# Pooled products one by one between the last pair's states; three output units ahead of the last pair, the fourth behind it

## The chip, the cores and the metric

The kernel runs on one core of one Trainium2 chip, as one program. The metric is the device time of one execution in microseconds. The core's engines are TensorE (PE in the rows; PEld is its weight load), VectorE (DVE), ScalarE (ACT), GpSimd (POOL) and SyncE (SP), which issues the transfers. They run side by side and meet at semaphores only.

## The reference, cut to what matters

Two transformer blocks run on 512 tokens of 1024 channels. The second block has a mixing layer whose input is split in two: 512 channels go through a recurrence over the sequence with 8 heads of 64 (`rwkv7_time_mix`), and 512 channels through averages over windows of 2, 4, 8 and 16 tokens (`multiscale_pool_mix`). Both halves are joined and multiplied by `w_out`, and the result is added to x. A feed-forward layer follows.

```python
    pooled = jnp.stack(outs, axis=2)
    mixed = jnp.einsum('bsgc,gcd->bsgd', pooled, w_pool.astype(f32))
    return (mixed.reshape(B, S, POOL_WIDTH) * pool_scale).astype(p.dtype)
...
        x = x + jnp.concatenate([y_rw, y_pool], axis=-1) @ w_out[l]
        x = x + 0.5 * swiglu(rms_norm_2(x, ffn2_norm[l]), ffn2_w_gate[l], ffn2_w_up[l], ffn2_w_down[l])
```

## The kernel before

**Units.** All large weights come as 233 units of 128x1024 float32 numbers (512 KB) through a ring of four slots. SyncE loads unit u to `raw`. ScalarE writes its rounded part to `w_hi` (`high_n`, L622, signals `hi_done`). GpSimd writes the rest to `w_lo` in four parts (`low`, L457, signals `lo_done`). TensorE then multiplies in three products, hi by hi, hi by lo and lo by hi (`three`, L1558 to L1560), and gives the slot back with `unit_used`. For `w_out`, unit U_OUT + m holds all weights of output tile m (128 output channels), in eight 128x128 blocks, one for each input tile k. `out_block(m, k, ...)` is one block, so three products of 128x512, that add up in PSUM bank m % 4.

**Input tiles of w_out.** Tiles k = 0 to 3 are the four pairs of heads of the recurrence. Tiles 4 to 7 are the four pool groups. Each is needed as `act_hi` (ScalarE: `mix_hi`, `pool_hi`) and `act_lo` (VectorE: `mix_lo`, `pool_lo`).

**The pairs.** The recurrence is worked out for pairs 0 to 3, in two lanes: pairs 0 and 2 in PSUM banks 0 to 3, pairs 1 and 3 in banks 4 to 7. `pair(p)` is written for each engine as a generator with 20 steps. Its steps 10 to 15 are the six states S1 to S6: TensorE multiplies (L1974), VectorE adds (L1444), and each state needs the one before it. Then come Y (L1978), the mean (L1982), the variance (L1986) and its spread over the channels, bc (L1991), between which VectorE and ScalarE work (`yc`, `sq`, `sd`, `inv`, `wide`, `yn`, `out`). Then `mix_hi(3)` and `mix_lo(3)` make input tile 3.

**Order of the work.** `in_turns` interleaves the lanes on each engine by hand. When the even lane has ended, the odd lane (pair 3) has its steps 11 to 20 left, and behind each of them the engine takes one step of its own generator `closing()`. What is left of `closing()` then runs on. On TensorE, `closing()` first issues the four products `w_pool` by `pooled` (float32, 128x512, L2019) behind step 11, which is S2. Its next three steps are empty. Then come the 28 blocks of units U_OUT to U_OUT + 3 for all k but 3, one behind each step of pair 3 and the rest in a row. Then TensorE closes the four units with k = 3, which needs pair 3, and goes on with units U_OUT + 4 to U_OUT + 7, eight blocks each. Unit U_OUT + 4 takes the slot of unit U_OUT.

ScalarE's `closing()` begins with the wait for pair 2's `out`, and prepares the units U_OUT to U_OUT + 2 behind `pool_hi(3)`. GpSimd's `closing()` (unchanged) makes the low parts of units U_OUT to U_OUT + 3 as they come, from the moment at which pair 3's step "Nb" is done. The pair's own buffers lie in the slots, so these units can't be written earlier. Behind the pairs, VectorE's `x2_new(m)` adds tile m to x once `unit_used` says that it is closed, ScalarE squares it (`x2_square`), and only then does ScalarE's queue come to `high_n(U_OUT + m + 4)`.

Of the kernel before, what the change touches and what calls it, by code (L numbers as in the profile page):

```python
# [21 lines left out]
KT = D // P  # L22
# [9 lines left out]
PAIRS = RW // P  # L32
CH = 64
NCH = T // CH
# [26 lines left out]
U_OUT = U_IN + len(IN_STARTS)  # L61
# [3 lines left out]
RING = 4  # L65
# [58 lines left out]
class Buffers:  # L124


    def __init__(self, bank, AA, MBR, MK, BT, KT, VT, GH, MT, TT, X, S, RP, OV):
# [5 lines left out]
PE_STEPS = (["tA", "tB", "tK", "tV", "LR", "K0", "K1", "AVa", "AVb", "G1a", "G1b", "Wa", "Wb", "GHa", "GHb", "RP", "OV", "MTa", "MTb", "Na", "Nb"]  # L133
            + [f"S{c}" for c in range(1, NCH - 1)] + ["Y", "mean", "var", "bc"])
VE_STEPS = (["LRa", "LRb", "K0a", "K0b", "K1a", "K1b", "AVb", "G1b", "Wb", "GHb", "RP", "MTa", "MTb", "Na", "Nb"]
            + [f"S{c}" for c in range(1, NCH - 1)] + ["Y", "yc", "inv", "yn", "out"])
# [11 lines left out]
def at(steps, pair, name):  # L148

    return pair // 2 * len(steps) + steps.index(name) + 1  # L150


LAG = 10
AHEAD_OF_SOLVE = 4


def in_turns(pair_program, closing):
# [8 lines left out]
    for first in (even, odd):  # L166
        for _ in range(AHEAD_OF_SOLVE):
            next(first)
    for _ in range(LAG):
        next(even)  # L170
# [8 lines left out]
def build(nc, a_vec, a_const, a_mask, a_x, a_xt, a_cs, a_wmod, a_w, a_lora, a_pool, out):  # L179
# [5 lines left out]
    with ExitStack() as ctx:  # L185
# [45 lines left out]
        def v(name, i=0, n=1):  # L231
            return vec[:, VEC[name] + i:VEC[name] + i + n]
# [92 lines left out]
        def sem(name):  # L325
            if name not in sems:
                sems[name] = ctx.enter_context(nc.semaphore(name))
            return sems[name]
# [18 lines left out]
        tensor_step, vector_step, scalar_step, pool_step = ([sem(f"{e}_step{i}") for i in range(2)] for e in ("tensor", "vector", "scalar", "pool"))  # L347
# [17 lines left out]
        def _(sp):  # L365
# [12 lines left out]
            def load_wm(i):  # L378

                n, flag, _, before = wm_place[i]  # L380
                if before is not None:
                    sp.wait_ge(sem("wm_used"), before + 1)
                sp.dma_start(wm_buf(n), a_wmod[i]).then_inc(wm_full[flag], 16)
# [229 lines left out]
        def _(act):  # L613
            def after(s, n):
                act.wait_ge(s, n)

            def high(u, slot, turn, first=False):

                act.wait_ge(raw_full[slot], 16 * (turn + 1))
                if not first:  # L620
                    act.wait_ge(unit_used, u - RING + 1)
                nc.scalar.activation(w_hi[:, slot, :], raw[:, slot, :], ACT.Copy).then_inc(hi_done, 1)  # L622

            def high_n(u):
                if u < NU:
                    high(u, u % RING, u // RING, u < RING)
# [304 lines left out]
            def mix_hi(p):  # L931
                nc.scalar.activation(act_hi[:, p, :], rG[:, p, :], ACT.Copy).then_inc(sem("mix_hi"), 1)

            def pool_hi(g):
                after(sem("pool_mm"), g + 1)
                nc.scalar.activation(act_hi[:, PAIRS + g, :], ps[:, g, :], ACT.Copy, scale=v("pool_scale", g)).then_inc(sem("pool_hi"), 1)

            def closing():

                act.wait_ge(vector_step[0], at(VE_STEPS, PAIRS - 2, "out"))  # L940
                mix_hi(0)

                act.wait_ge(vector_step[1], at(VE_STEPS, PAIRS - 3, "out"))
                mix_hi(1)
                yield
                mix_hi(2)
                pool_hi(0)
                yield
                pool_hi(1)
                pool_hi(2)  # L950
                yield

                act.wait_ge(tensor_step[1], at(PE_STEPS, PAIRS - 1, "OV"))
                assert U_OUT % RING == 3
                pool_hi(3)
                for u in range(U_OUT, U_OUT + RING - 1):
                    high_n(u)
                    yield
                act.wait_ge(vector_step[1], at(VE_STEPS, PAIRS - 1, "Y"))
                high_n(U_OUT + RING - 1)  # L960

            in_turns(pair, closing)
            act.wait_ge(vector_step[1], at(VE_STEPS, PAIRS - 1, "out"))
            mix_hi(PAIRS - 1)
# [47 lines left out]
        def _(ve):  # L1012
# [10 lines left out]
            def tt(o, a, b, op, name=None):  # L1023
                chain(nc.vector.tensor_tensor(o, a, b, op), name)  # L1024

            def stt(o, a, s, b, op0, op1, name=None):
                chain(nc.vector.scalar_tensor_tensor(o, a, s, b, op0, op1), name)  # L1027
# [440 lines left out]
            def mix_lo(p):  # L1468
                after(sem("mix_hi"), p + 1)
                tt(act_lo[:, p, :], rG[:, p, :], act_hi[:, p, :].bitcast(f32), SUB, "mix_lo")  # L1470

            def pool_lo(g):
                after(sem("pool_hi"), g + 1)
                stt(act_lo[:, PAIRS + g, :], ps[:, g, :], v("pool_scale", g), act_hi[:, PAIRS + g, :].bitcast(f32), MUL, SUB, "pool_lo")

            def closing():
                yield
                mix_lo(0)
                mix_lo(1)
                yield  # L1480
                mix_lo(2)
                pool_lo(0)
                yield
                pool_lo(1)
                pool_lo(2)
                yield

                ve.wait_ge(tensor_step[1], at(PE_STEPS, PAIRS - 1, "Nb"))
                pool_lo(3)

            in_turns(pair, closing)
            mix_lo(PAIRS - 1)

# [43 lines left out]
            n = 0  # L1537
# [16 lines left out]
        def _(pe):  # L1554
            after = pe.wait_ge

            def three(o, wh, wl, xh, xl, start, stop, **check):
                nc.tensor.matmul(o, wh, xh, start=start, stop=False, **check)  # L1558
                nc.tensor.matmul(o, wh, xl, start=False, stop=False, **check)  # L1559
                return nc.tensor.matmul(o, wl, xh, start=False, stop=stop, **check)  # L1560

            def blk(slot, b):
                return w_hi[:, slot, b * P:(b + 1) * P], w_lo[:, slot, b * P:(b + 1) * P]
# [432 lines left out]
            def out_block(m, k, start, stop):  # L1996

                u = U_OUT + m
                if start:
                    after(lo_done, u + 1)  # L2000
                    if m < RING:
                        after(sem("pool_lo"), m + 1)
                    else:
                        after(sem("x2_new"), m - 3)
                if m == 0:
                    after(*((sem("mix_lo"), k + 1) if k < PAIRS else (sem("pool_lo"), k - PAIRS + 1)))
                last = three(ps[:, m % 4, :], *blk(u % RING, k), act_hi[:, k, :], act_lo[:, k, :], start, stop)
                if stop and m < KT - 1:
                    last.then_inc(unit_used, 1)
                return last  # L2010


            others = [k for k in range(KT) if k != PAIRS - 1]

            def closing():
                after(sem("pooled"), len(WINDOWS))
                pe.wait_ge(vector_step[0], at(VE_STEPS, PAIRS - 2, "out"))
                for g in range(len(WINDOWS)):
                    nc.tensor.matmul(ps[:, g, :], w_pool[:, g, :], pooled[:, g, :], start=True, stop=True).then_inc(sem("pool_mm"), 1)  # L2019
                for _ in range(4):  # L2020
                    yield

                n = 0
                for m in range(RING):
                    for k in others:
                        out_block(m, k, k == 0, False)
                        n += 1
                        if n < NCH - 1 or n % 5 == 0:
                            yield

            in_turns(pair, closing)


            for m in range(KT - 1):
                if m >= RING:
                    for k in others:
                        out_block(m, k, k == 0, False)
                out_block(m, PAIRS - 1, False, True)
            for k in range(KT):
                out_block(KT - 1, k, k == 0, k == KT - 1).then_inc(sem("act_free"), 1)  # L2040
# [81 lines left out]
```

## Time and profile before

| | us |
|---|---|
| runs: median (lowest to highest) | 1588.21 (1586.77 to 1591.11) |
| profiled execution: its time | 1597.47 |
| profiled execution: its span | 1595.7 |
| PE, DVE, ACT, POOL busy | 1499.1, 565.7, 508.6, 761.8 |
| mean granted TensorE clock | 0.969 |

The span runs from the first to the last instruction of the profiled execution; 1.8 us of its time lie outside it. All positions in the rows are us from the start of the span. The clock is a share of full speed: 1.00 is 2.4 GHz and 0.50 is 1.2 GHz.

### The profile page before, as it was taken

What the parts mean: (1) busy time and instruction counts of PE and PEld (TensorE: products, weight loads), DVE (VectorE), ACT (ScalarE), POOL (GpSimd) and SP (SyncE); (2) the same over time, 40 slices, a digit from 0 to 9 for tenths busy, and PEclk for the clock granted to TensorE, in tenths of its full rate; (3) what the DMA queues carried; (4) which work ended last, traced back from release to release, by engine and by line L of the source; (5) the groups of instructions that cost most, each with busy time, mean ns of one, the idle gap of its engine ahead of it and who ended that gap; (6) DMA issues with size and microseconds to landing.
All of it is one profiled execution on the core that took longest, in us unless ns stands there. A gap on an engine that the chain in (4) does not pass through costs nothing.

```text
span 1595.7 us, 20172 instructions
## 1 busy us (share of the span) xinstructions
PE 1499.1 (94%) x7230; PEld 1237.9 (78%) x7230; DVE 565.7 (35%) x794; ACT 508.6 (32%) x706; POOL 761.8 (48%) x1013
## 2 busy tenths in 40 slices
PE   5797999999999999999999999689889999999997
PEld 4674788888888788888888687578667888888887
DVE  6795342222003832222001647845523322222003
ACT  4424333333123333223222664122313322322112
POOL 0372464555555655455455636160034745545553
PEclk9888999999999999999999999899879999999999
DMA  8871234222222232232232221000012323223221
GB/s 310 318 264 40 93 132 145 98 96 96 97 100 79 93 105 92 92 105 92 96 102 92 72 73 63 9 2 1 1 53 93 117 94 105 91 93 105 93 79 53
DMA packets 44545, 156.90 MB, mean 98 GB/s; under 512 B 4944, under 2 KB 7376, under 8 KB 44240
## 3 DMA queue, kind: packets, MB, share of 16 engines
q1 hardware_dynamic: 44496, 156.22, 28.5%
q8 instruction: 33, 0.54, 0.1%
q14 instruction: 16, 0.13, 0.0%
HBM read 154.11 MB, written 2.10 MB: 98 GB/s over the span
## 4 chain that ended last, share of the span: by engine, by line
PE 77%; issue 11%; DVE 7%; POOL 4%; ACT 1%; DVEq 0%; POOLq 0%; ACTq 0%
PE ps L1558 23%; PE ps L1560 23%; PE ps L1559 23%; POOL w_lo L457 4%; DVE act_lo L1027 1%; DVE tri_p L1024 1%; DVE tri_x L1024 1%; PE ps L1918 1%; DVE xT L1027 1%; PE ps L1978 1%; DVE mid_sq L1027 0%; PE ps L1925 0%; PE ps L1931 0%; PE ps L1974 0%; PE ps L1965 0%
## 5 line engine op out<-in xcount | busy, mean ns | idle before, releaser
L457 POOL TENSOR_TENSOR w_lo<-raw,w_hi 128x256 fp32r<-128x256 f32 x932 | 694.3, 778 | 750.3 <-ACT w_hi L622 750.0
L1558 PE MATMUL ps<-act_hi,w_hi 128*128 128x512 f32 x1328 | 532.0, 401 | 20.5 <-DVE act_lo L1024 11.3
L1559 PE MATMUL ps<-act_lo,w_hi 128*128 128x512 f32 x1328 | 523.1, 394 | 0.0
L1560 PE MATMUL ps<-act_hi,w_lo 128*128 128x512 f32 x1328 | 522.9, 394 | 0.0
L622 ACT ACTIVATE w_hi<-raw 128x1024 fp32r<-128x1024 f32 x233 | 245.0, 1055 | 451.9 <-PE ps L1560 424.0
L1558 PEld LDWEIGHTS ps<-act_hi,w_hi 128*128 128x128 f32 x1328 | 253.3, 191 | 85.8 <-issue 14.9
L1559 PEld LDWEIGHTS ps<-act_lo,w_hi 128*128 128x128 f32 x1328 | 253.5, 191 | 53.9 <-issue 2.7
L1560 PEld LDWEIGHTS ps<-act_hi,w_lo 128*128 128x128 f32 x1328 | 253.0, 190 | 53.6
L1558 PE MATMUL ps<-hid_hi,w_hi 128*128 (+3 forms) x584 | 220.4, 377 | 9.0 <-DVE hid_lo L1027 5.9
L1559 PE MATMUL ps<-hid_lo,w_hi 128*128 (+3 forms) x584 | 219.9, 376 | 0.0
L1560 PE MATMUL ps<-hid_hi,w_lo 128*128 (+3 forms) x584 | 219.8, 376 | 0.0
L1558 PEld LDWEIGHTS ps<-hid_hi,w_hi 128*128 128x128 f32 x584 | 111.2, 190 | 29.3 <-issue 9.6
L1560 PEld LDWEIGHTS ps<-hid_hi,w_lo 128*128 128x128 f32 x584 | 111.1, 190 | 19.7
L1559 PEld LDWEIGHTS ps<-hid_lo,w_hi 128*128 128x128 f32 x584 | 111.2, 190 | 19.6
L717 ACT ACTIVATE hid_hi<-g_buf 128x512 f32 (+1 forms) x66 | 41.8, 633 | 257.9 <-DVE g_buf L1167 217.5
L1164 DVE TENSOR_TENSOR u_buf<-ps,rstd 128x512 f32<-128x512 f32 x44 | 30.4, 691 | 182.6 <-PE ps L1560 182.6
L1169 DVE TENSOR_TENSOR hid_lo<-g_buf,hid_hi 128x512 f32 (+1 forms) x66 | 48.1, 730 | 58.7 <-ACT hid_hi L717 58.7
L1162 DVE TENSOR_TENSOR g_buf<-ps,rstd 128x512 f32<-128x512 f32 x44 | 30.4, 691 | 94.0 <-PE ps L1560 93.6
L715 ACT ACTIVATE g_buf<-g_buf 128x512 f32<-128x512 f32 x66 | 41.1, 622 | 48.9 <-DVE g_buf L1154 37.3
L1152 DVE SCALAR_TENSOR_TENSOR g_buf<-ps,vec,g_buf 128x511 f32<-128x511 f32 x22 | 16.5, 750 | 108.2 <-ACT g_buf L713 108.2
L1027 DVE SCALAR_TENSOR_TENSOR xT<-ps,mods,xT 128x512 f32<-128x512 f32 x16 | 12.0, 751 | 113.9 <-PE ps L1560 113.5
L1523 DVE SCALAR_TENSOR_TENSOR xT<-ps,xT 128x256 f32<-128x256 f32 x16 | 6.8, 424 | 110.0 <-PE ps L1560 110.0
(264 smaller groups left out, 1150.9 us busy)
## 6 DMA issues: line engine op xcount, KB each, us to landing
raw<-weight_units SPq DMA_DIRECT2D x233, 512.0 KB, 3.2
wm_ring<-mod_units SPq DMA_DIRECT2D x16, 512.0 KB, 5.9
wm_mid<-mod_units SPq DMA_DIRECT2D x16, 512.0 KB, 6.6
wm_early<-mod_units SPq DMA_DIRECT2D x8, 512.0 KB, 9.3
wm_late<-mod_units SPq DMA_DIRECT2D x8, 512.0 KB, 5.4
x_tok<-tokens SPq DMA_DIRECT2D x4, 512.0 KB, 6.4
xT<-tokens_by_channel SPq DMA_DIRECT2D x1, 2048.0 KB, 14.9
result<-act_out SPq DMA_DIRECT2D x16, 128.0 KB, 1.8
```

The source lines that it names most:

```text
L457: ins = nc.gpsimd.tensor_tensor(w_lo[:, slot, c], raw[:, slot, c], w_hi[:, slot, c].bitcast(f32), SUB)
L622: nc.scalar.activation(w_hi[:, slot, :], raw[:, slot, :], ACT.Copy).then_inc(hi_done, 1)
L715: nc.scalar.activation(g_buf[:, q, :], g_buf[:, q, :], ACT.Silu).then_inc(s["silu"], 1)
L717: nc.scalar.activation(hid_hi[:, bass.ds(j * T, T)], g_buf[:, q, :], ACT.Copy).then_inc(s["hid_hi"], 1)
L1024: chain(nc.vector.tensor_tensor(o, a, b, op), name)
L1027: chain(nc.vector.scalar_tensor_tensor(o, a, s, b, op0, op1), name)
L1162: nc.vector.tensor_tensor(g, gate, rstd[:, :], MUL).then_inc(s["act_in"], 1)
L1164: nc.vector.tensor_tensor(u_, val, rstd[:, :], MUL).then_inc(s["val_read"], 1)
L1169: nc.vector.tensor_tensor(hid_lo[:, bass.ds(j * T, T)], g, hid_hi[:, bass.ds(j * T, T)].bitcast(f32), SUB).then_inc(s["hid_lo"], 1)
L1558: nc.tensor.matmul(o, wh, xh, start=start, stop=False, **check)
L1559: nc.tensor.matmul(o, wh, xl, start=False, stop=False, **check)
L1560: return nc.tensor.matmul(o, wl, xh, start=False, stop=stop, **check)
```

## The change

TensorE issues the four pooled products one by one, behind S2, S3, S4 and S5. It waits for pair 2's `yn` in place of its `out`. The blocks for k other than 3 are issued for three units only (`BEFORE_MIX = 3`, 21 blocks), two behind each step of pair 3 from S6 on. These three units are closed with k = 3, and the fourth is done behind them like the later ones, all of its eight blocks in a row. ScalarE prepares unit U_OUT first, U_OUT + 1 and U_OUT + 2 between the `mix_hi` and `pool_hi`, and U_OUT + 3 one step of pair 3 later than before: behind `sd`, no longer behind `sq`. VectorE's `mix_lo` and `pool_lo` are spread by one step each.

```diff
+BEFORE_MIX = 3
...
             def closing():
 
+                assert U_OUT % RING == 3
+                act.wait_ge(tensor_step[1], at(PE_STEPS, PAIRS - 1, "OV"))
+                high_n(U_OUT)
                 act.wait_ge(vector_step[0], at(VE_STEPS, PAIRS - 2, "out"))
                 mix_hi(0)
 
                 act.wait_ge(vector_step[1], at(VE_STEPS, PAIRS - 3, "out"))
                 mix_hi(1)
                 yield
+                high_n(U_OUT + 1)
                 mix_hi(2)
                 pool_hi(0)
                 yield
+                high_n(U_OUT + 2)
                 pool_hi(1)
+                yield
                 pool_hi(2)
                 yield
-
-                act.wait_ge(tensor_step[1], at(PE_STEPS, PAIRS - 1, "OV"))
-                assert U_OUT % RING == 3
                 pool_hi(3)
-                for u in range(U_OUT, U_OUT + RING - 1):
-                    high_n(u)
-                    yield
+                yield
+                yield
+                yield
                 act.wait_ge(vector_step[1], at(VE_STEPS, PAIRS - 1, "Y"))
                 high_n(U_OUT + RING - 1)
...
             def closing():
                 yield
                 mix_lo(0)
+                yield
                 mix_lo(1)
+                pool_lo(0)
                 yield
                 mix_lo(2)
-                pool_lo(0)
-                yield
                 pool_lo(1)
+                yield
                 pool_lo(2)
                 yield
-
                 ve.wait_ge(tensor_step[1], at(PE_STEPS, PAIRS - 1, "Nb"))
                 pool_lo(3)
...
             def closing():
                 after(sem("pooled"), len(WINDOWS))
-                pe.wait_ge(vector_step[0], at(VE_STEPS, PAIRS - 2, "out"))
+                pe.wait_ge(vector_step[0], at(VE_STEPS, PAIRS - 2, "yn"))
                 for g in range(len(WINDOWS)):
                     nc.tensor.matmul(ps[:, g, :], w_pool[:, g, :], pooled[:, g, :], start=True, stop=True).then_inc(sem("pool_mm"), 1)
-                for _ in range(4):
                     yield
 
-                n = 0
-                for m in range(RING):
-                    for k in others:
-                        out_block(m, k, k == 0, False)
-                        n += 1
-                        if n < NCH - 1 or n % 5 == 0:
-                            yield
+                for n, (m, k) in enumerate((m, k) for m in range(BEFORE_MIX) for k in others):
+                    out_block(m, k, k == 0, False)
+                    if n % 2:
+                        yield
 
             in_turns(pair, closing)
 
 
-            for m in range(KT - 1):
-                if m >= RING:
-                    for k in others:
-                        out_block(m, k, k == 0, False)
+            for m in range(BEFORE_MIX):
+                out_block(m, PAIRS - 1, False, True)
+            for m in range(BEFORE_MIX, KT - 1):
+                for k in others:
+                    out_block(m, k, k == 0, False)
                 out_block(m, PAIRS - 1, False, True)
```

## Rows read from the trace of the kernel before

**Rows 1.** The page: busy time, and the chain that ended last.

```profile
PE 1499.1 (94%) x7230; PEld 1237.9 (78%) x7230; DVE 565.7 (35%) x794; ACT 508.6 (32%) x706; POOL 761.8 (48%) x1013
...
PE 77%; issue 11%; DVE 7%; POOL 4%; ACT 1%; DVEq 0%; POOLq 0%; ACTq 0%
```

**Rows 2.** Stretches of the span: length, busy (instructions) per engine, clock, DMA.

```profile
core 0: us, PE busy (x) PEld busy (x) DVE busy (x) ACT busy (x) POOL busy (x), PEclk, DMA share, GB/s
1143.90:1147.56 3.66, 2.38 (x5) 1.35 (x6) 1.51 (x4) 1.67 (x3) 0.00 (x0) 0.54 0.00 0
1147.56:1150.97 3.41, 3.41 (x6) 1.34 (x5) 0.00 (x0) 1.37 (x2) 0.00 (x0) 0.50 0.00 0
1150.97:1154.38 3.41, 1.74 (x8) 0.88 (x6) 2.08 (x5) 2.99 (x4) 0.53 (x1) 0.99 0.00 0
1154.38:1157.13 2.75, 1.50 (x4) 0.93 (x4) 2.64 (x5) 1.22 (x2) 2.75 (x5) 0.51 0.01 3
1157.13:1168.60 11.47, 11.01 (x35) 8.03 (x34) 3.77 (x6) 1.58 (x2) 6.15 (x10) 0.50 0.42 139
1168.60:1174.86 6.26, 6.26 (x20) 5.00 (x21) 2.40 (x4) 1.35 (x3) 2.10 (x4) 0.50 0.25 84
1174.86:1192.35 17.49, 17.49 (x78) 14.30 (x76) 2.08 (x3) 1.23 (x3) 0.00 (x0) 1.00 0.00 0
1192.35:1196.25 3.90, 0.16 (x2) 0.00 (x1) 1.94 (x3) 3.25 (x5) 3.29 (x5) 0.89 0.00 0
1196.25:1202.30 6.05, 6.05 (x14) 4.79 (x15) 2.22 (x3) 1.90 (x3) 6.05 (x8) 0.51 0.47 146
1202.30:1215.50 13.20, 13.20 (x59) 10.89 (x58) 2.77 (x4) 3.17 (x4) 8.71 (x13) 1.00 0.38 133
```

**Rows 3.** TensorE's timeline: start, length, line, tiles, count, idle before and releaser.

```profile
1145.76 6.21 PE L2019 MATMUL ps<-pooled,w_pool 128*128 128x512 f32 x8
...
1156.36 0.80 PE L1974 MATMUL ps<-S,MT 128*128 128x128 f32 x2 [1.25 <-DVE S L1444]
...
1158.58 3.09 PE L1978 MATMUL ps<-RP,S 128*128 128x64 f32 x14
...
1163.35 2.08 PE L1982 MATMUL ps<-rB,const 128*128 128x512 f32 x2 [0.30 <-DVE rB L1450]
...
1170.02 2.05 PE L1991 MATMUL ps<-const,rK 128*128 128x128 f32 x8
...
1196.25 0.80 PE L1558 MATMUL ps<-act_hi,w_hi 128*128 128x512 f32 x1 [3.74 <-POOL w_lo L457]
```

**Rows 4.** ScalarE's timeline, same columns.

```profile
1135.95 0.62 ACT L927 ACTIVATE rK<-norms 128x512 f32<-128x512 f32 x1
...
1152.66 2.94 ACT L622 ACTIVATE w_hi<-raw 128x1024 fp32r<-128x1024 f32 x3
...
1166.72 1.04 ACT L622 ACTIVATE w_hi<-raw 128x1024 fp32r<-128x1024 f32 x1
...
1191.84 1.04 ACT L622 ACTIVATE w_hi<-raw 128x1024 fp32r<-128x1024 f32 x1
```

**Rows 5.** VectorE's timeline, same columns.

```profile
1144.05 0.69 DVE L1465 TENSOR_TENSOR rG<-rB,rG 128x512 f32<-128x512 f32 x1
...
1154.21 0.91 DVE L1024 TENSOR_TENSOR act_lo<-rG,act_hi 128x512 fp32r<-128x512 f32 x1
...
1175.07 0.69 DVE L1024 TENSOR_TENSOR act_lo<-rG,act_hi 128x512 fp32r<-128x512 f32 x1 [0.70 <-ACT act_hi L932]
1190.58 1.42 DVE L1024 TENSOR_TENSOR xT<-ps,xT 128x512 f32<-128x512 f32 x2 [14.81 <-PE ps L1560]
...
1218.80 6.56 DVE L1027 SCALAR_TENSOR_TENSOR act_lo<-xT,vec,act_hi 128x512 fp32r<-128x512 f32 x7 [0.87 <-ACT act_hi L974]
```

**Rows 6.** GpSimd's timeline, same columns.

```profile
1153.85 8.73 POOL L457 TENSOR_TENSOR w_lo<-raw,w_hi 128x256 fp32r<-128x256 f32 x12 [80.98 <-ACT w_hi L622]
...
1192.96 12.45 POOL L457 TENSOR_TENSOR w_lo<-raw,w_hi 128x256 fp32r<-128x256 f32 x16 [22.27 <-ACT w_hi L622]
```

More of the change, by code:

```diff
@@ L1478, in closing @@
                 mix_lo(0)
+                yield
                 mix_lo(1)
+                pool_lo(0)
                 yield
                 mix_lo(2)
-                pool_lo(0)
+                pool_lo(1)
                 yield
-                pool_lo(1)
                 pool_lo(2)
```

## The prediction

> **What bounds the kernel now.** I read the page first. TensorE is busy for 94% of the span and carries 77% of the chain that ended last [rows 1], so a change pays if it takes TensorE's idle time away or lets it run at the higher clock. Next I cut the stretch around the change into windows at the places where the granted clock changes [rows 2]. Three things are to be seen there. First, between 1150.97 and 1157.13 TensorE is busy for 1.74 + 1.50 = 3.24 of 6.16 us: it waits for VectorE's additions between the states S3 to S6 (1.25 us before S6 alone, [rows 3]). Second, from 1154.38 to 1174.86, 20.5 us, it runs at 0.50, so 1.2 GHz, although it is busy nearly throughout. Third, from 1192.35 to 1196.25 it waits for GpSimd's `w_lo` of unit U_OUT + 4 [rows 2, 3], and then runs at 0.51 for 6.05 us.
>
> What stands behind the clock can be read off the same rows. It fell to 0.5 when work became sparse (1143.9, 1154.4, and with the wait at 1192 to 1196). It rose twice behind gap-free stretches: at 1150.97, after TensorE had been busy without a gap since 1145.97 with the pooled products, and at 1174.86, after 6.26 us without a gap. In the 11.47 us before 1168.60 the small gaps sum to 0.46 us, and the small products of Y and of the variance lie in it [rows 2, 3]; it did not rise. By the Trainium skill, page "TensorE: Matmul & The Clock Gate", section "Part 1: The HAM clock gate", the default state is the lower clock and activity releases it; the trace agrees, and where a stretch falls decides which clock it gets.
>
> Prices: at full clock 17.49 us hold about 77 products, 0.227 each, 0.68 us for a block of three. At 1.2 GHz 6.05 us hold 14, 0.432 each, 1.30 us for a block [rows 2]. The four pooled products took 6.2 us, 5.0 of them at half clock and 1.0 at full [rows 2, 3], so 1.75 us each at half and 0.88 at full clock. Work at the other clock than in its row is halved or doubled (an estimate from these).
>
> **The change part by part.** *Wait on `yn` in place of `out`:* nothing. `out` ends at 1144.05 + 0.69 = 1144.74 [rows 5], and S2, which stands ahead of the products, waits for an addition that VectorE does behind it.
>
> *Pooled products between the states.* Each product (1.75 or 0.88 us) now covers the 0.35 us addition and its latency that TensorE waited for. I lay the new order out from S2. I let it start 0.3 us later than before, as ScalarE, idle from 1136.57 [rows 4], now makes w_hi of U_OUT at once, and GpSimd starts its low part at about 1142.3, beside VectorE's `out`. The row for such company is 0.91 us for an operation that takes 0.69 alone, and 6.56 us for seven that take 0.75 [rows 5]. By the Trainium skill, page "SBUF — State Buffer", section "Who interferes with whom", an instruction of VectorE with two SBUF inputs and one of GpSimd that reads SBUF block each other, the second waiting for the first; by full blocking each of the handful of such operations here would lose up to one GpSimd part, 12.45/16 = 0.78 us [rows 6], some 3 us in all. The rows show 0.2 to 0.4 each, and I take those.
>
> From 1146.3 at half clock: product 1.75, S3 0.5, product 1.75, S4 0.5, that is 1150.8, 4.5 us without a gap. I expect the clock to rise about here, near 1151. Then product 0.88 and S5 to 1152.1, product to 1153.0. S6 waits for the S5 addition, in front of which VectorE has S4's, `mix_lo(1)` and `pool_lo(0)`: 0.1 + 0.35 + 0.91 + 0.75 + 0.35 behind 1150.8, 1153.3. S6 to 1153.6, two blocks to 1155.0. Y waits for the S6 addition behind `mix_lo(2)` and `pool_lo(1)`, 1155.3, and takes half of 3.09 us: 1156.8. Two blocks 1158.2, mean (half of 2.08) 1159.2, two blocks 1160.6, variance 0.9, 1161.5, two blocks 1162.8. Then bc waits for ScalarE: `sd` 0.3, the w_hi of U_OUT + 3 that now stands there 1.04, `wide` 0.63, 1163.5; bc to 1164.5. Thirteen of the 21 blocks are left: 8.84 us, 1173.4.
>
> *Tile 3.* Before, `mix_lo(3)` ended at 1175.76, 5.7 us behind the start of bc at 1170.02 [rows 3, 5]. Now that would be 1169.2, 4.2 us ahead of need. So issuing only 21 blocks ahead of it costs nothing; without the 13 blocks it would cost 4.7 us.
>
> *Three units closed, the fourth behind them.* Closings 2.04 us, 1175.4; fourth unit 8 blocks, 5.44 us, 1180.8. Before, the w_lo of U_OUT + 4 came 3.3 (1196.25 less 1192.96) + 1.12 + 1.26 = 5.7 us behind the start of the first addition to x at 1190.58 [rows 3 to 6], and only four closings lay in between. Now the first closing ends at 1174.1, the addition starts at about 1174.3, w_lo is there at 1180.0, and the fourth unit covers all of it, with 0.8 us to spare. The idle 3.9 us go. So does what they brought: 6.05 us at half clock would take 3.0 at full. GpSimd needs 12.45/4 = 3.1 us a unit [rows 6], TensorE 5.44, so it does not fall behind later. The DMAs of the units behind U_OUT + 3 start earlier, when the low parts are done; the DMA share stays under 0.5 in these rows. *The three further units* 24 blocks, 16.3 us: 1197.1.
>
> **Sum.** In the profile of before unit U_OUT + 6 is closed at 1215.5, now at 1197.1: 18.4 us. Of it the stall is 3.9, the half clock behind it 3.0, and 11.5 come from the stretch up to 1192. All that follows depends on this end and is unchanged, so the gain reaches the end of the program. The profiled execution took 1597.5 us, 9.3 more than the median of the runs shown; I carry the difference over. The moment at which the clock rises will vary: each us that it comes later than 1151 costs about 0.42 us (18.4 less 8.3 of the first rival, over 24 us). I take it as 3 us late: 17 us, 1588.2 - 17 = **1571**.
>
> **The rivals.**
> *The clock stays low until 1174.86, as before.* For it speaks that the states' products are short and have their own waits, and that the broken stretch before 1168.60 did not raise the clock. Against it that pooled products and states follow each other without a gap from 1146.3 on. Then the order runs at half clock: products and states to 1155.3, two blocks 1157.9, Y 1160.9, blocks 1163.5, mean 1165.5, blocks 1168.1, variance 1169.9, blocks 1172.5, bc 1174.5. That is 8.3 blocks at 1174.86, where before had 32 - 17.49/0.68 = 6.3. The gain is 2 x 0.68 = 1.4, plus 3.9 and 3.0: 8.3 us, 1580.
> *It rises somewhere in the blocks (1157 to 1168)*, which are now less broken: 8.3 + 0.42 x (6 to 18) = 11 to 16 us, 1572 to 1577.
> *The stall does not go* (w_lo of U_OUT + 4 late after all, since TensorE arrives at it faster and the spare is 0.8 us). With the clock low too, only 1.4 us are left: 1587, no change. With the clock high, 18.4 - 6.9 = 11.5: 1577.
> *Slower: pair 3's tail becomes the bound.* The w_hi of U_OUT + 3 stands between `sd` and `wide`, and the cover behind bc is 13 blocks, where all 28 had been available. If the way from bc to `mix_lo(3)` took over 8.84 us, TensorE would wait, and at a wait of 3 to 4 us it would drop to half clock, another 3 us. To lose 5 us net against even the 8.3 us case the tail must take 8.84 + 8.3 + 5 - 3 = 19 us or more. It took 5.7. Price then 1593 and up.
>
> **How the numbers follow.** High clock from about 1151: 0.57 (1568 to 1574). Rise in the blocks: 0.18 (1572 to 1577). Low until 1175: 0.13 (1580). Stall stays, no change: 0.08 (1587). Slower: 0.04 (1593). Runs of before differ by 4 us, and within 0.3% (4.8 us) this measurement can't tell a change from none. The range goes from 1566, the first case with nothing lost (18.4) and the scatter of the runs, to 1582, which takes in the third. Faster by over 0.3%: the first three, 0.88; within: 0.08; slower: 0.04.
>
> **What would show it.** After: no idle time between S3 and S6 but that before S6; a granted clock of 1.00 from about 1151 until past 1200; blocks of 0.68 us between the steps of pair 3; no wait of TensorE for `w_lo` at the first block of U_OUT + 4; `mix_lo(3)` done some us ahead of the first closing. The prediction is wrong if the clock stays at 0.50 in the blocks, or falls again in them, or if TensorE waits for `mix_lo(3)` or for U_OUT + 4.

## The result, and the profile after

The changed kernel took 1578.39 us (median of 10 runs, 1573.74 to 1581.36), the kernel before 1591.32 us (10 runs, 1586.00 to 1599.91). The ratio is 0.9918, 95% interval 0.9899 to 0.9937, so 13 us faster, 10 to 16 by the interval. Two more measurements gave 0.9928 and 0.9902. Faster had been forecast, by 17 us to 1571; 1578 lies in the range of 1566 to 1582. Of the 7.4 us between 1571 and 1578.39, 4 are a gain forecast too large. The other 3 are the base: the forecast started from the median of three runs, 1588.21, and that of ten is 1591.32.

The profiled executions show a larger gain than the runs. The one of after took 1578.12 us against 1597.47. Its windows, with the columns of [rows 2]:

```profile
1142.03:1145.31 3.28, 1.08 (x4) 0.89 (x5) 2.54 (x3) 0.99 (x2) 2.84 (x3) 0.65 0.00 0
1145.31:1149.70 4.39, 4.39 (x10) 2.32 (x10) 1.86 (x3) 3.56 (x6) 3.15 (x4) 0.50 0.33 119
1149.70:1152.49 2.79, 2.34 (x9) 1.03 (x9) 2.54 (x5) 1.72 (x3) 2.79 (x5) 0.98 0.54 167
1152.49:1162.54 10.05, 9.60 (x51) 7.10 (x50) 4.49 (x9) 2.40 (x5) 1.38 (x2) 1.00 0.18 60
1162.54:1180.30 17.76, 17.76 (x82) 14.87 (x83) 7.08 (x10) 5.27 (x7) 6.92 (x10) 1.00 0.11 31
1180.30:1196.20 15.90, 15.90 (x71) 13.16 (x71) 4.95 (x6) 4.75 (x6) 14.01 (x19) 1.00 0.48 164
```

The clock falls at about the place where it did before (0.65 in the window around S1), rises at 1149.7, once products and states have run without a gap since S2, and then stays at 1.00 to the end of the stretch. In [rows 2] the 20.5 us from 1154.38 to 1174.86 were at half clock. The 3.9 us wait and the 6.05 us at half clock behind it have no counterpart here. From the start of S1 to the addition of tile U_OUT + 6 to x, 1215.77 - 1143.29 = 72.5 us had passed; now it is 1196.49 - 1142.08 = 54.4, 18.1 us less. The 18.4 us of the prediction's sum were for this stretch. That addition is the seventh, since the first row of additions holds two; the expectations below call it the sixth and mean the same row. The ends of the stretch before, and its start after:

```profile
1143.29 0.49 PE L1974 MATMUL ps<-S,MT 128*128 128x128 f32 x2 [0.97 <-DVE S L1434]
1215.77 0.69 DVE L1024 TENSOR_TENSOR xT<-ps,xT 128x512 f32<-128x512 f32 x1 [3.29 <-PE ps L1560]
```

```profile
1142.08 0.49 PE L1978 MATMUL ps<-S,MT 128*128 128x128 f32 x2 [0.97 <-DVE S L1438]
```

TensorE's timeline after, with the columns of [rows 3]:

```profile
1144.72 0.80 PE L1978 MATMUL ps<-S,MT 128*128 128x128 f32 x2 [2.15 <-DVE S L1448]
1145.31 1.92 PE L2023 MATMUL ps<-pooled,w_pool 128*128 128x512 f32 x2
1147.02 0.63 PE L1978 MATMUL ps<-S,MT 128*128 128x128 f32 x2
...
1150.56 0.38 PE L1978 MATMUL ps<-S,MT 128*128 128x128 f32 x2
1150.78 1.02 PE L2023 MATMUL ps<-pooled,w_pool 128*128 128x512 f32 x2
1152.25 0.49 PE L1978 MATMUL ps<-S,MT 128*128 128x128 f32 x2 [0.45 <-DVE S L1448]
...
1157.13 1.02 PE L1986 MATMUL ps<-rB,const 128*128 128x512 f32 x2
...
1162.54 1.16 PE L1995 MATMUL ps<-const,rK 128*128 128x128 f32 x8 [0.33 <-ACT rK L928]
```

Each state now follows its product without idle time, except S6 (0.45 us), as forecast. The mean takes 1.02 where it took 2.08, bc 1.16 where it took 2.05 [rows 3]. The wait ahead of S2 has grown to 2.15 us from 1.40, as these rows of before show, of TensorE and of VectorE:

```profile
1145.18 0.79 PE L1974 MATMUL ps<-S,MT 128*128 128x128 f32 x2 [1.40 <-DVE S L1444]
1143.26 0.75 DVE L1027 SCALAR_TENSOR_TENSOR rB<-rB,vec,rBonus 128x512 f32<-128x512 f32 x1
```

VectorE's timeline after says why:

```profile
1142.06 1.09 DVE L1031 SCALAR_TENSOR_TENSOR rB<-rB,vec,rBonus 128x512 f32<-128x512 f32 x1
1143.19 1.10 DVE L1469 TENSOR_TENSOR rG<-rB,rG 128x512 f32<-128x512 f32 x1
1144.32 0.35 DVE L1448 SCALAR_TENSOR_TENSOR S<-ps,pchunk,S 128x128 f32<-128x128 f32 x1
...
1166.89 0.69 DVE L1028 TENSOR_TENSOR act_lo<-rG,act_hi 128x512 fp32r<-128x512 f32 x1 [0.70 <-ACT act_hi L933]
...
1196.49 0.69 DVE L1028 TENSOR_TENSOR xT<-ps,xT 128x512 f32<-128x512 f32 x1 [3.29 <-PE ps L1564]
```

Pair 2's last two operations stand ahead of S1's addition, and take 1.09 and 1.10 us here; they took 0.75 (the row above) and 0.69 before [rows 5]. They run beside GpSimd's first low part, which now starts at 1141.20:

```profile
1141.20 3.67 POOL L458 TENSOR_TENSOR w_lo<-raw,w_hi 128x256 fp32r<-128x256 f32 x4 [69.52 <-PE ps L1970]
...
1175.76 15.79 POOL L458 TENSOR_TENSOR w_lo<-raw,w_hi 128x256 fp32r<-128x256 f32 x20 [10.84 <-ACT w_hi L623]
```

`mix_lo(3)` is done at 1167.58, 5.0 us behind the start of bc. TensorE has 13 blocks left behind bc and comes to the first closing at about 1172.4, 4.8 us later, so tile 3 stays hidden. The low parts of U_OUT + 4 begin at 1175.76, while TensorE works on the fourth unit, and TensorE does not wait for them. The w_hi of U_OUT + 3, now between `sd` and `wide`, shows no price: bc waits for ScalarE for 0.33 us, and it waited for 0.45 and 0.46 us in the two later profiles of the kernel before.

### The profile page after: what moved, and what is told of

Its sections match the earlier page's. It is cut to its first block, busy times and chain, and to the rows that moved or that the text cites. A ratio compares the mean times of both kernels' runs of the same rounds, so it can differ in the third digit from the quotient of the medians.

```text
span 1576.3 us, 20170 instructions
## 1 busy us (share of the span) xinstructions
PE 1486.0 (94%) x7230; PEld 1229.4 (78%) x7230; DVE 569.3 (36%) x794; ACT 508.9 (32%) x706; POOL 765.7 (49%) x1013
## 4 chain that ended last, share of the span: by engine, by line
PE 78%; issue 9%; DVE 7%; POOL 4%; ACT 1%; DVEq 0%; POOLq 0%; ACTq 0%
PE ps L1562 23%; PE ps L1564 23%; PE ps L1563 23%; POOL w_lo L458 4%; DVE act_lo L1031 1%; DVE tri_p L1028 1%; DVE tri_x L1028 1%; PE ps L1922 1%; DVE xT L1031 1%; PE ps L1978 1%; DVE mid_sq L1031 0%; PE ps L1929 0%; PE ps L1935 0%; PE ps L1876 0%; PE ps L1982 0%
## 5 line engine op out<-in xcount | busy, mean ns | idle before, releaser
L1562 PE MATMUL ps<-act_hi,w_hi 128*128 128x512 f32 x1328 | 526.4, 396 | 15.9 <-DVE act_lo L1028 11.4
L1562 PEld LDWEIGHTS ps<-act_hi,w_hi 128*128 128x128 f32 x1328 | 250.1, 188 | 80.2 <-issue 13.7
L1563 PEld LDWEIGHTS ps<-act_lo,w_hi 128*128 128x128 f32 x1328 | 250.3, 189 | 52.6 <-issue 2.4
```

## The experiments

All ratios are to the kernel before, in runs on the same chip; us are (1 - ratio) x 1590. "Stretch" is the time from the start of S1 to the seventh addition to x (tile U_OUT + 6) in the one profiled execution. In v1 and v2 one pooled product stands ahead of S1 and is not in it.

| kernel | ratio (95%) | us against before | stretch in its profile |
|---|---|---|---|
| before | 1 | 0 | 72.5; second and third profile: 65.4, 67.2 |
| changed | 0.9918 (0.9899 to 0.9937) | -13 | 54.4 |
| changed, a0 | 0.9928 (0.9906 to 0.9950) | -11 | 54.4 |
| changed, a1 | 0.9902 (0.9872 to 0.9932) | -16 | 54.4 |
| products alone, e1 | 0.9967 (0.9950 to 0.9984) | -5 | 60.0 |
| three units alone, e2 | 0.9948 (0.9928 to 0.9969) | -8 | 56.9 |
| three units, filled, e3 | 0.9934 (0.9913 to 0.9956) | -10 | 56.4 |
| one unit ahead, e4 | 0.9941 (0.9920 to 0.9962) | -9 | 62.0 |
| before, filled, e5 | 0.9968 (0.9948 to 0.9987) | -5 | 63.4 |
| from S1 on, v1 | 0.9868 (0.9846 to 0.9890) | -21 | 48.8 |
| the same, v2 | 0.9873 (0.9846 to 0.9901) | -20 | 48.8 |

**The changed kernel again.** No edit.

> The changed kernel itself, beside the others on the same chip. In the one profiled execution of each, the change took 18 us out of the stretch from S1 to the closing of unit U_OUT + 6; the timed runs so far moved by 12.9 us only (ratio 0.9918). Theory A: the profiled execution of the old kernel was one with a long stretch at half clock, others have a shorter one; then again 11 to 15 us faster here, with a granted clock that stays at 0.974 or above. Theory B: the 12.9 was chance and the true gain is 17 to 18 us.

Measured: 1578.55 us, 11 us faster. The stretch in its profile is 54.4 us again. Three measurements gave 11, 13 and 16 us. The intervals of the first two end at 15 and 16, so a true gain of 17 to 18 us is unlikely; only the third's interval (11 to 20) takes it in. The first theory, that the profiled execution of before was an unlucky one, was left to test.

**The products alone.**

```diff
-BEFORE_MIX = 3
+BEFORE_MIX = 4
```

> One part alone: the pooled products one by one between the states, as in the changed kernel, but four output units ahead of the last pair, as before (28 blocks, then four closings). Theory A (stretch and stall add up): the clock rises at about 1151 and stays up in the blocks; TensorE waits again some 3.9 us for w_lo of U_OUT + 4 and then runs about 6 us at half clock. So 18.4 - 6.9 = 11 us faster than before in the profile, 5 to 9 us in the timed runs. Theory B (the stall was all that cost anything on average): within 2 us of before.

Measured: 1584.33 us, 5 us faster than before. The windows of its profile, from the first product on:

```profile
1142.03:1150.79 8.76, 8.27 (x24) 4.34 (x23) 5.92 (x11) 5.32 (x8) 6.88 (x8) 0.75 0.36 121
1150.79:1176.70 25.91, 25.46 (x123) 20.39 (x122) 7.44 (x12) 4.12 (x7) 2.81 (x4) 1.00 0.12 41
1176.70:1180.51 3.81, 0.08 (x1) 0.00 (x0) 1.94 (x3) 3.17 (x5) 3.28 (x5) 1.00 0.00 0
1180.51:1184.00 3.49, 3.49 (x8) 2.79 (x9) 2.23 (x3) 1.91 (x3) 3.49 (x4) 0.51 0.46 150
```

The clock stays up through the 28 blocks. Then the wait for U_OUT + 4 is there (3.73 us idle in front of its first block) and with it 3.5 us at half clock. Against the changed kernel the stretch is 60.0 - 54.4 = 5.6 us longer, where the prediction had 6.9 for wait and half clock; by the runs of the same chip it is (0.9967 - 0.9928) x 1590 = 6.2 us, and the two intervals leave some 4 us either way. That term is borne out, and the second theory of this run, that the products bring nothing, falls: the interval ends at 0.9984, 2.5 us faster than before.

**The three units alone.**

```diff
                 for g in range(len(WINDOWS)):
                     nc.tensor.matmul(ps[:, g, :], w_pool[:, g, :], pooled[:, g, :], start=True, stop=True).then_inc(sem("pool_mm"), 1)
-                    yield
+                for _ in range(4):
+                    yield
```

> The other part alone: three units ahead of the last pair and the fourth behind it, but the four pooled products all behind S2, as before. ScalarE and VectorE keep the order of the changed kernel. Theory A: TensorE waits between S3 and S6 as before, the clock falls there and stays at 0.5 into the blocks; no wait for U_OUT + 4. About 8 us faster than before (3.9 for the wait, 3.0 for the half clock behind it, 1.4 for the idle time), 5 us slower than the whole change. Theory B: as fast as the whole change, 13 us.

Measured: 1582.36 us, 8 us faster than before, and 3.8 us slower than the changed kernel of the same chip (1578.55), where 5 had been expected. Its profile, from the first product on:

```profile
1147.60:1153.29 5.69, 5.69 (x10) 2.39 (x10) 0.35 (x1) 4.60 (x7) 4.45 (x7) 0.60 0.33 104
1153.29:1158.89 5.60, 3.13 (x15) 2.06 (x13) 5.00 (x10) 0.71 (x2) 1.07 (x2) 1.00 0.48 176
1158.89:1178.10 19.21, 18.75 (x94) 15.12 (x94) 6.06 (x10) 3.00 (x5) 2.81 (x4) 1.00 0.09 29
```

From 1153.29 to 1158.89 TensorE is busy for 3.13 of 5.60 us only, as in [rows 2] between 1150.97 and 1157.13. But this time the clock did not fall. What had been expected of this profile, half clock into the blocks, was wrong, though the time was near what had been expected. So states as sparse as these are followed by half clock in the profiled execution of before and not in this one. The stretch is 56.9 - 54.4 = 2.5 us longer than in the changed kernel, and TensorE idles for 5.60 - 3.13 = 2.47 us in the window from S3 on: with three units ahead, the profiles show the idle time as what the spread products save, and no half clock.

**Filled gaps behind three products.** The fourth pooled product (index 3 in the code) is computed three times, twice for nothing.

```diff
-                for g in range(len(WINDOWS)):
+                for g in range(3):
                     nc.tensor.matmul(ps[:, g, :], w_pool[:, g, :], pooled[:, g, :], start=True, stop=True).then_inc(sem("pool_mm"), 1)
+                yield
+                for _ in range(2):
+                    nc.tensor.matmul(ps[:, 3, :], w_pool[:, 3, :], pooled[:, 3, :], start=True, stop=True)
                     yield
+                nc.tensor.matmul(ps[:, 3, :], w_pool[:, 3, :], pooled[:, 3, :], start=True, stop=True).then_inc(sem("pool_mm"), 1)
+                yield
```

> The kernel with three units ahead and the pooled products behind S2, but of these only the first three; behind S3 and S4 the fourth product is computed twice for nothing (same operands, same bank, nobody reads it), and behind S5 for good. It does two products of 128x512 float32 more than the changed kernel or the kernel with the products together. Theory A (filled gaps keep the clock up, and that is what the spread products bring): faster than the kernel with the products together, by 3 to 6 us, despite more work; 1 to 3 us slower than the changed kernel, for two products at 0.9 to 1.75 us. Theory B (idle time itself, not the clock): no faster than the kernel with the products together, rather 1 to 3 us slower.

Measured: 1580.94 us, 1.4 us faster than the kernel with the products together despite two products more, where the first theory had 3 to 6. The intervals overlap by far, and in the profile of neither did the clock fall (stretches 56.4 and 56.9), so this pair does not separate the theories.

**The kernel before, profiled twice more.** No edit, one execution each.

> The kernel before, unchanged, for a second profile. Theory A (the half clock through the blocks is there in some executions only, and the profile of before showed one of them): with some luck the clock stays at 1.00 behind 1151 here, or rises much earlier than 1175; the stretch from S1 to the sixth addition to x then takes 62 to 64 us in place of 72.5. Theory B (it is there always): 72 us again.

> As b1_look, a third profile of the kernel before, with the same expectations: 62 to 64 us from S1 to the sixth addition to x if the clock stays up, 72 if it falls, something between if it rises in the midst of the blocks.

The second profiled execution took 1587.27 us, the third 1591.41. Windows of the second, from the first pooled product on:

```profile
1142.39:1151.15 8.76, 5.29 (x18) 2.61 (x16) 5.08 (x10) 6.53 (x9) 3.28 (x5) 0.98 0.00 1
1151.15:1161.00 9.85, 9.39 (x26) 6.41 (x26) 3.76 (x6) 0.80 (x2) 5.45 (x8) 0.50 0.46 160
1161.00:1183.30 22.30, 21.85 (x103) 17.88 (x103) 4.47 (x7) 3.35 (x6) 2.80 (x4) 1.00 0.07 24
```

and of the third, from its first block on:

```profile
1156.80:1165.90 9.10, 8.35 (x26) 5.62 (x26) 3.32 (x6) 0.73 (x2) 5.46 (x8) 0.62 0.52 174
1165.90:1188.40 22.50, 22.04 (x103) 17.91 (x103) 4.47 (x7) 3.57 (x6) 2.80 (x4) 1.00 0.07 24
```

The instructions and their order are those of [rows 2], but the half clock behind the states lasts 9.9 us in the second profile, some 7 in the third (a mean of 0.62 over 9.10 us is (1 - 0.62) x 9.10/0.5 = 6.9), and 20.5 in the first. In the second the pooled products ran at full clock too. The stretches are 65.4, 67.2 and 72.5 us. Their mean is 68.4, 14.0 more than the changed kernel's 54.4, near the 11 to 16 measured, though three executions are few for a mean. In the 15 runs of before beside the first experiments, the fastest, 1585.13, had a mean clock of 0.976 and the slowest, 1596.41, one of 0.969. That is 0.007 x 1590 = 11.1 us of full clock lost, and the runs lie 11.3 us apart. The other runs agree: over all 43 runs of before beside the experiments, each chip's mean taken off, time and mean clock have a correlation of -0.87, and a run is some 1.0 us shorter for each 0.001 more. The first profile had 0.969 as well. A mean clock does not say where the clock was low, and other stretches vary too: in the three profiles of before it was 0.91, 0.90 and 0.88 from 1000 to 1100 us.

**One unit ahead.**

```diff
-BEFORE_MIX = 3
+BEFORE_MIX = 1
```

> The changed kernel with one output unit ahead of the last pair in place of three: 7 blocks, then the closing with k = 3, then units U_OUT + 1 and on in full. Theory A (the blocks are a cover for pair 3's tail, and what is not covered is paid): the 7 blocks are used up before bc; behind bc TensorE waits some 4.0 us for mix_lo(3) (5.0 from the start of bc to its end in the changed kernel, less 0.9 for bc itself), and may drop to half clock for another 3 us. 4 to 7 us slower than the changed kernel, still 4 to 8 us faster than before. Theory B (TensorE has slack at this place, the cover is not needed): within 2 us of the changed kernel.

Measured: 1583.18 us, ratio 0.9941 against the changed kernel's 0.9918, 0.9928 and 0.9902, so 2 to 6 us slower than it. Slower by 4 to 7 us had been expected. In its profile the stretch is 7.6 us longer. TensorE at the place:

```profile
1165.65 0.80 PE L1562 MATMUL ps<-act_hi,w_hi 128*128 128x512 f32 x1 [3.74 <-DVE act_lo L1028]
1166.24 0.63 PE L1563 MATMUL ps<-act_lo,w_hi 128*128 128x512 f32 x1
1166.67 0.63 PE L1564 MATMUL ps<-act_hi,w_lo 128*128 128x512 f32 x1
```

It waits 3.74 us for `mix_lo(3)`, 4.0 had been worked out, and then its products take 0.43 us each (starts 1166.24, 1166.67) until 1171:

```profile
1165.65:1171.20 5.55, 5.55 (x13) 4.38 (x14) 0.69 (x1) 1.57 (x2) 1.41 (x3) 0.51 0.00 1
```

These 5.55 us of half clock cost 2.7. The blocks are a cover that is needed: the wait of 3.74 us is as long as five to six of the 13 that stand behind bc in the changed kernel.

**The kernel before, filled.** Three products are added into bank 6, nothing is moved.

```diff
-                for _ in range(4):
+                yield
+                for _ in range(3):
+                    nc.tensor.matmul(ps[:, 6, :], w_pool[:, 0, :], pooled[:, 0, :], start=True, stop=True)
                     yield
```

> The kernel before with work added and nothing else moved: behind S3, S4 and S5, where TensorE waits for VectorE, it computes one product of 128x512 float32 each into bank 6, which nobody reads until bc overwrites it. At full clock the three take 2.65 us, about what TensorE idles there (3.2 us in the profiles of before). Theory A (the idle time between the states matters mostly because the clock falls behind it): the clock that rises in the pooled products stays up through the blocks; 3 to 6 us faster than before, though nothing was taken away. Theory B (the idle time itself is what the change saves, the clock is chance): no faster than before, 0 to 2 us slower.

Measured: 1586.65 us (12 runs) against 1590.92 (17 runs), ratio 0.9968, interval 0.9948 to 0.9987: some 5 us faster with more work. The added products are the L2022 rows of its timeline:

```profile
1153.52 0.39 PE L1974 MATMUL ps<-S,MT 128*128 128x128 f32 x2
1153.74 1.02 PE L2022 MATMUL ps<-pooled,w_pool 128*128 128x512 f32 x2
1154.60 0.38 PE L1974 MATMUL ps<-S,MT 128*128 128x128 f32 x2
...
1156.38 1.02 PE L2022 MATMUL ps<-pooled,w_pool 128*128 128x512 f32 x2
1158.06 0.49 PE L1974 MATMUL ps<-S,MT 128*128 128x128 f32 x2 [0.65 <-DVE S L1444]
```

and its windows:

```profile
1152.20:1158.84 6.64, 5.48 (x17) 2.29 (x17) 4.73 (x9) 4.21 (x5) 3.29 (x5) 0.98 0.00 1
1158.84:1188.10 29.26, 27.40 (x128) 21.36 (x128) 7.89 (x13) 4.29 (x7) 8.24 (x12) 1.00 0.22 72
1191.86:1208.58 16.72, 16.72 (x74) 13.85 (x75) 5.39 (x8) 5.07 (x7) 15.26 (x20) 1.00 0.46 158
```

The clock is up from 1152.5 on and stays up through the blocks; the stretch is 63.4 us, where before had 65.4, 67.2 and 72.5. Not all of that lies at the edit. The half clock behind the 3.7 us wait for U_OUT + 4 is missing in this profile too (1.00 in the last window, 0.51 over 6.05 us in [rows 2]), and the edit does not touch that wait. From S1 to the start of the wait it takes 42.9 us, where before took 43.1, 45.4 and 49.1, so 2.9 less than their mean.

The runs say more than this one profile. The 12 of this kernel have a mean clock of 0.9766, the 17 of before one of 0.9736. The difference is 0.0030 x 1590 = 4.8 us of full clock, and the mean times are 4.8 us apart (1586.5 and 1591.3). The idle time between the states is filled with useless work but for 0.86 us ahead of S5 and S6, so it isn't saved; what is saved is half clock. The theory that only idle time counts falls.

**A further version.** Products from in front of S1 on, pair 2's last operations behind the additions of S1 and S2, `mix_hi` and `mix_lo` of pairs 0 and 1 in the waits of pair 2, three w_hi at once, the first blocks behind S4 and S5. The edit is cut to its main parts.

```diff
+                if p == PAIRS - 1:
+                    after(sem("pooled"), len(WINDOWS))
+                    pe.wait_ge(vector_step[0], at(VE_STEPS, PAIRS - 2, "yn"))
+                    pool_product(0)
                 ve_did("Nb")
...
                     did(f"S{c}", nc.tensor.matmul(bank((c + 1) % 2)[:, 0:P], b.MT[:, c, :], b.S[:, c - 1, :], start=True, stop=True))
+                    if p == PAIRS - 1 and c < len(WINDOWS):
+                        pool_product(c)
                     yield
...
                     did(f"S{c}", nc.vector.scalar_tensor_tensor(b.S[:, c, :], bank((c + 1) % 2)[:, 0:P], pchunk[:, p, c:c + 1], b.S[:, c, :], MUL, ADD))
+                    if p == PAIRS - 1 and c == 1:
+                        biased(PAIRS - 2)
+                    if p == PAIRS - 1 and c == 2:
+                        gated_out(PAIRS - 2)
                     yield
...
-                high_n(U_OUT)
+                for u in range(U_OUT, U_OUT + RING - 1):
+                    high_n(u)
+                pool_hi(0)
+                pool_hi(1)
+                pool_hi(2)
                 act.wait_ge(vector_step[0], at(VE_STEPS, PAIRS - 2, "out"))
...
                 mix_hi(2)
...
                 pool_hi(3)
```

`biased` and `gated_out` are the two operations behind `yn`.

> A version that goes on from the changed kernel. In its profile TensorE still idles 2.15 us ahead of S2, where VectorE finishes pair 2 between the additions of S1 and S2, and runs at half clock from 1143 to 1149. Here the pooled products start one step of pair 3 earlier, ahead of S1, and follow behind S1, S2 and S3; pair 2's last two operations stand behind the additions of S1 and S2; mix_hi and mix_lo of pairs 0 and 1 are made while the engines wait for pair 2's variance and bc; all three w_hi come at once; and the first blocks of w_out stand behind S4 and S5. Theory A (idle time and half clock there add up like those of the change): TensorE never falls to half clock in this stretch, 4 to 6 us faster than the changed kernel, 15 to 18 us faster than before. Theory B (VectorE is the bound between S1 and S6, its additions come no earlier): within 2 us of the changed kernel.

> The version that starts the pooled products ahead of S1, once more and on the same chip as the changed kernel. Its first run came out 8 us faster than the changed kernel by the ratios to before. Theory A: 6 to 9 us faster than the changed kernel again, of it 5.6 us in the stretch that the profiles show (54.4 against 60.0 us from the start of pair 3's MT products to the sixth addition to x). Theory B: only what VectorE and ScalarE save by earlier mix operations, 1 to 3 us.

> The changed kernel once more, beside the further version on the same chip: 11 to 13 us faster than before under either theory.

Measured: 1570.59 us, ratio 0.9868, in the first run; in the second 1572.10, 0.9873, beside the changed kernel at 1575.68, 0.9902. So it is 20 to 21 us faster than before, and by the second run 3.6 us (medians) to 4.6 us (ratios) faster than the changed kernel, between the 6 to 9 and the 1 to 3 of that run's two theories. Against before, 15 to 18 had been expected. The two ratios of the first rounds are 8 us apart, but on different chips. Its parts were not run alone, so which of them brings how much stays open. Its windows, from pair 3's MT products on:

```profile
1133.18:1148.03 14.85, 14.33 (x88) 10.59 (x88) 11.40 (x22) 4.88 (x7) 9.67 (x12) 1.00 0.23 71
1148.03:1157.50 9.47, 9.10 (x52) 7.13 (x51) 1.94 (x5) 2.36 (x4) 1.61 (x3) 1.00 0.18 57
1157.50:1187.54 30.04, 30.04 (x134) 24.82 (x134) 12.02 (x16) 10.01 (x13) 19.81 (x26) 1.00 0.32 105
```

The granted clock is 1.00 in all of them. From that start to the seventh addition it takes 54.4 us, the changed kernel 1196.49 - 1136.51 = 60.0.

## Why the prediction was right, and where it was off

**Right, step by step.** The wait on `yn` brought nothing: S2 stands behind an addition in both. The states are hidden behind the products, S6 alone waits (0.45 us). The clock rose at 1149.7, 1151 had been forecast. Tile 3 is hidden with 4.8 us to spare where 4.2 had been worked out, and the run with one unit ahead showed that its cover is needed. The wait for U_OUT + 4 is gone; it is worth 5.6 us in a profile and 6.2 (some 4 either way) in the runs, with its half clock, where 6.9 stood in the sum. The sum for the stretch was 18.4 us, and between the two profiles it is 18.1.

**Off: the term for the stretch up to 1192.** It stood at 11.5 us (of the 18.4). In the runs it is some 3 to 5 us: the products alone bring 5 (3 to 8 by the interval), and added to three units 3.2 ((0.9948 - 0.9928) x 1590, with some 5 either way). The step that failed is the one that says "I carry the difference over". The profiled execution of before was 9.3 us over the median of three runs, 6.2 over that of ten, and these 9.3 us were taken for a constant. They were in good part half clock in the very stretch that the change mends: the two further executions were 10.2 and 6.1 us shorter, 7.1 and 5.3 of it there. The rows of one execution gave the length of the half clock as 20.5 us; it varies with the execution, from some 7 to 20.5, and there was none behind states as sparse in the profile with three units alone. The gain is what it is on average, 14.0 by three profiles. The prediction let the clock's moment vary for the changed kernel only (3 us late) and not for the kernel before.

**Luck.** The first case came true, a high clock from about 1151 on, but its band was 1568 to 1574, and 1578 lies outside it, between the bands of two cases that did not come. The range held the time because it had been stretched to 1582 for the case of a low clock until 1175.

**The rivals.** The clock staying low in the blocks and the stall that stays did not come. The slower one, pair 3's tail, is real as a mechanism: it shows with a cover of seven blocks in place of 21, and then costs 2 to 6 us. The contention of VectorE with GpSimd was sized at 0.3 us ahead of S2. Measured is 0.75 us more wait there (2.15 against 1.40), all of it in the two operations (0.34 and 0.41). The rows that the prediction names show 0.2 us for an operation (0.91 against 0.69, and 6.56/7 against 0.75), not the "0.2 to 0.4" that it reads there.

**Left open.** Whether filled gaps help where three units are ahead isn't separated from noise. That the wait on `yn` brought nothing is read from the rows; no run has it alone. What decides how long an execution of before stays at half clock isn't shown, and three profiles are few for a mean.

## What to carry to other kernels

Idle time of TensorE between small dependent steps costs twice: the time itself, and the half clock that may follow it into dense work. Where such products are at hand, put independent ones one by one into the gaps, not in a row in front of them. Where a ring of slots feeds TensorE, close and give back units while one more prepared unit is left to cover the next one's preparation. And if the profiled execution lies well above the median, look for what differs before its rows are taken for the typical run.

## What the runs showed of the hardware

The same instructions in the same order ran for 20.5, about 10 and about 7 us at half clock behind the same states in three executions of one kernel. Adding three products that nobody reads, some 2.65 us of work at full clock, made the kernel 5 us faster (2 to 8). Behind a wait of 3.7 us for the same unit, U_OUT + 4, products ran at half clock for 6.05 us in one execution, for 3.5 in another, and not at all in a third. VectorE's operations on two operands in SBUF took 1.09 and 1.10 us beside GpSimd's subtraction where they took 0.75 and 0.69 without it, while its additions for the states, which read PSUM, stayed at 0.35 us beside it. So these two engines can slow each other without a semaphore between them.
